# The FFN's down projection and the final norm, moved from channels on partitions to tokens on partitions

## The reference, cut to what matters

```python
h  = rmsnorm(x, norm2_g)
up = causal_dwconv(h @ ffn_w_up, conv_w, conv_b)        # 2048 -> 2 * 6144, three taps
gate, val = split(up, 2)
x  = x + (gelu(gate) * val) @ ffn_w_down                 # 6144 -> 2048
out = x * rsqrt(mean(x * x, axis=-1) + 1e-6) * final_g   # over the 2048 channels
```

## Time and profile before

| what | value |
|---|---|
| runs | 2379.47, 2385.78, 2387.15 us |
| profiled execution | 2380.07 us, span 2378.3 us |
| mean granted TensorE clock | 0.986 of full speed |
| TensorE busy | 2286.2 us (96%) |
| VectorE, ScalarE, GpSimd busy | 1311.4 us (55%), 1043.1 us (44%), 266.3 us (11%) |
| HBM read, written | 427.85 MB, 6.29 MB |

### The profile page before, as it was taken

The page is one execution under the profiler, slowest core; times in us unless marked ns, Lnnn a source line. Parts: engine busy times, 40 slices in busy tenths (PEclk is TensorE's granted clock), DMA queues, the critical chain, the costliest instruction groups (busy, mean ns, idle before and its releaser), DMA issues.

```text
span 2378.3 us, 30943 instructions
## 1 busy us (share of the span) xinstructions
PE 2286.2 (96%) x12255; PEld 1857.3 (78%) x12255; DVE 1311.4 (55%) x2114; ACT 1043.1 (44%) x1606; POOL 266.3 (11%) x333
## 2 busy tenths in 40 slices
PE   5889999999999999999999998999999999999998
PEld 2457777777777866778888886888888888888887
DVE  2443533332323264545676767667765777567764
ACT  2222333332322155445554465456544555355543
POOL 1000000000001022100010424111100110001111
PEclk9889999999999999999999999999999999999999
DMA  9764433345655465734566544555555565565552
GB/s 367 275 244 176 142 123 133 127 136 168 221 183 177 160 236 182 260 106 146 185 192 214 176 142 156 172 186 187 187 194 186 187 195 187 192 188 187 190 189 81
DMA packets 346895, 436.16 MB, mean 183 GB/s; under 512 B 13848, under 2 KB 269280, under 8 KB 345856
## 3 DMA queue, kind: packets, MB, share of 16 engines
q1 hardware_dynamic: 341376, 413.19, 52.5%
q0 software_dynamic: 3280, 15.86, 1.8%
q10 hardware_dynamic: 2096, 5.15, 0.6%
HBM read 427.85 MB, written 6.29 MB: 183 GB/s over the span
## 4 chain that ended last, share of the span: by engine, by line
PE 87%; DVE 5%; ACT 3%; DMA 3%; issue 1%; POOL 1%; SPq 0%; ACTq 0%; POOLq 0%
PE ps L1287 30%; PE ps L1288 16%; PE ps L1262 5%; PE ps L1264 5%; PE ps L1263 5%; PE ps L1282 5%; PE ps L1284 5%; PE ps L1283 5%; PE ps L1243 3%; DVE SPL L1726 2%; ACT SPL L1491 2%; DMA RAW<-in_w_in_dram 1%; PE ps L1336 1%; PE ps L1353 1%; DMA RAW<-in_ada_w_dram 1%
## 5 line engine op out<-in xcount | busy, mean ns | idle before, releaser
L1287 PE MATMUL ps<-HS,SPL 128*128 128x512 f32 x3456 | 1215.8, 396 | 14.5 <-DVE SPL L1726 9.6
L1726 DVE TENSOR_TENSOR SPL<-RAW,SPL 128x1024 fp32r<-128x1024 f32 x592 | 751.6, 1273 | 603.2 <-ACT SPL L1491 600.5
L1288 PE MATMUL ps<-HS,SPL 128*128 128x256 f32 x3456 | 968.4, 280 | 0.0
L1491 ACT ACTIVATE SPL<-RAW 128x1024 fp32r<-128x1024 f32 x592 | 621.7, 1055 | 475.1 <-PE ps L1288 281.3
L1287 PEld LDWEIGHTS ps<-HS,SPL 128*128 128x128 f32 x3456 | 649.5, 188 | 167.4 <-DVE SPL L1726 8.4
L1288 PEld LDWEIGHTS ps<-HS,SPL 128*128 128x128 f32 x3456 | 654.4, 189 | 1.9 <-issue 1.7
L1262 PE MATMUL ps<-SPL,HS 128*128 128x512 f32 x576 | 250.5, 435 | 21.1 <-ACT XT L1533 6.7
L1264 PE MATMUL ps<-SPL,HS 128*128 128x512 f32 x576 | 230.8, 401 | 0.0
L1263 PE MATMUL ps<-SPL,HS 128*128 128x512 f32 x576 | 230.8, 401 | 0.0
L1282 PE MATMUL ps<-HS,SPL 128*128 128x512 f32 x480 | 195.4, 407 | 1.2 <-DVE HS L1882 1.2
L1284 PE MATMUL ps<-HS,SPL 128*128 128x512 f32 x480 | 187.7, 391 | 0.0
(11 more groups left out here) (272 smaller groups left out, 1701.3 us busy)
## 6 DMA issues: line engine op xcount, KB each, us to landing
RAW<-in_w_in_dram SPq DMA_DIRECT2D x208, 512.0 KB, 5.8
RAW<-in_ada_w_dram SPq DMA_DIRECT2D x192, 512.0 KB, 4.9
RAW<-in_ffn_w_up_dram SPq DMA_DIRECT2D x192, 512.0 KB, 3.6
RAW<-in_w_out_dram SPq DMA_DIRECT2D x96, 512.0 KB, 4.4
RAW<-in_ffn_w_down_dram SPq DMA_DIRECT2D x96, 512.0 KB, 3.3
x_spill<-XT POOLq DMA_DIRECT2D x2, 2048.0 KB, 15.4
XT<-x_spill POOLq DMA_DIRECT2D x1, 4096.0 KB, 17.4
MM<-in_x_dram ACTq DMA_DIRECT2D x2, 1024.0 KB, 10.8
```

What stands on the lines that cost most here:

```text
L1287: mm(PS[b][:, :], wr, hh, start=k == 0, stop=False, skip_group_check=True)
L1288: m = mm(PS[b][:, 256:512], wl, hh[:, 0:256], start=False, stop=k == KT - 1, skip_group_check=True)
L1491: act(SPL[:, (n - 1) % NSPL, 0, :], raw_of(i), ACT.Copy).then_inc(s_hi, 1)
L1726: tt(w[:, 1, :], raw_of(s["i"]), w[:, 0, :].bitcast(F32), ALU.subtract).then_inc(s_lo, 1)
```

## The change: the diff

The down projection is put in tm form: four groups of 512 output channels for each round, eight chunks each, each with two banks (one for either half of the tokens). Its eviction `rows_add` adds one bank of 128 tokens by 512 channels to x. For that, x is turned at the start of the FFN: eight steps `x_turn`, put into `low`, each of four transposes into bank 7 and one copy by VectorE into `XO`, the second half of `XT`. `final_g` is no longer loaded as a row at the start; GpSimd's queue loads it at the start of the FFN, spread over all partitions (1 MB written), into `GF`, the last quarter of `MM`.

In round 2 ScalarE squares each row block of three of the four groups and sums along the row in the same instruction, and GpSimd multiplies it by the gains. The last four chunks are walked twice, first for tokens 0 to 127 and then for 128 to 255, so that the first half's norm can run beside the second half's matmuls. Of the tail there are left, for each half: the sum into x, the square, one small add, the power on GpSimd, the scaling (group 3 on VectorE with its gains, group 2 on VectorE, groups 0 and 1 on ScalarE) and four stores. The sum over partitions, the diagonal, the scaling by columns and the transposes at the end go.

```diff
-        OT = [MM[:, 2048 * t:2048 * (t + 1)] for t in range(2)]
+        XO = [XT[:, 4096 + 2048 * t:4096 + 2048 * (t + 1)].rearrange("p (g c) -> p g c", g=4) for t in range(2)]
+        GF = MM[:, 6144:8192].rearrange("p (g c) -> p g c", g=4)
...
-        c_fin2 = col(0, 80, vec(I["final_g_2"]), 16)
...
+        def x_turn(g, t):
+            def f():
+                s = put("x_turn", g=g, t=t, after=use(7), last=[y["x_done"], y["down"]], res=tick("res"))
+                bank_last[7] = [(s_res, s["res"])]
+            return f
...
+        def rows_add(r, g, banks):
+            def f():
+                ready = [rows_sum(g, t, banks[t], multiplied()) for t in range(2)]
+
+                def square(t):
+                    y["squared"] = rows_square(g, t, ready[t])
+                    put("rows_gain", g=g, t=t, last=[y["squared"]])
+                if r == 2:
+                    hi.extend([lambda: square(0), lambda: square(1)])
+            return f if (r, g) != (2, 3) else None
...
-            downs = [c for i in range(8) for c in group("fm", ("down", r), Wd, i * 256, alt(i), x_add(2 * i, alt(i), sq3 if r == 2 else None))]
+            downs = [c for i in range(4) for c in group("tm", ("down", r), Wd, i * 512, alt(i), rows_add(r, i, alt(i)), TILES[:2])]
...
+        y["x_done"] = (s_res, count["res"])
+        put("final_gain_in", last=[y["down"]])
+        low.extend([x_turn(g, t) for g in range(4) for t in range(2)])
         for r in range(3):
             need["down", r] = lambda k, r=r: [act_ready[r, k]]
-            run_chunks(marks[10 + r])
+            run_chunks(marks[10 + r] - (4 if r == 2 else 0))
             y["down"] = multiplied()
         flush(hi)
-        cnt = sq3.count(4)
-        slot, bank_last[4] = rstd_a(2, 1.0 / D, PS[4][:, 0:2], [cnt])[0], [(s_ms, count["rstd_a"])]
-        rs3 = rstd_b(2, slot, 5)
-        for k in range(KT):
-            put("final", k=k, ready=rs3, after=use(*[2 * (k // 4 % 2) + t for t in range(2)]) if k % 4 == 0 else {})
...
+        put("rows_mean", last=[y["squared"]])
+        first = at["pos"]
+        for t in range(2):
+            for kc in range(4):
+                run_ahead()
+                ks = range(2 * (4 + kc), 2 * (4 + kc) + 2)
+                put("mm", i=first + kc, c=chunks[first + kc], inputs={k: need["down", 2](k) for k in ks}, after={}, banks=[t], end=t == 1, src=None)
+                at["pos"] += t
+                at["used"] += t
+            ready = rows_sum(3, t, alt(3)[t], multiplied() if t else (s_part, tick("part")))
+            put("rows_norm", t=t, last=[rows_square(3, t, ready)], power=tick("power"), res=tick("res", 2) - 1)
...
+                elif s["kind"] == "rows_norm":
+                    t = s["t"]
+                    for sm, v, g in ((s_fine, 2 * t + 1, 0), (s_res, s["res"], 3), (s_fine, 2 * t + 2, 1), (s_res, s["res"] + 1, 2)):
+                        e.wait_ge(sm, v)
+                        e.dma_start(out[0, t * 128:(t + 1) * 128, g * 512:(g + 1) * 512], XO[t][:, g, :]).then_inc(s_out, 16)
...
+                elif kind == "x_turn":
+                    t = s["t"]
+                    for sm, v in new(*s["last"]):
+                        e.wait_ge(sm, v)
+                    for i in range(4):
+                        m = turn(PS[7][:, i * 128:(i + 1) * 128], XV[:, 0, 4 * s["g"] + i, t * 128:(t + 1) * 128], IDN[:, :])
+                    m.then_inc(s_fint, 1)
...
+                    act(T(s["slot"]), XO[t][:, g, :], ACT.Square, scale=D ** -0.5, accum_out=STAT[:, 4 * t + g:4 * t + g + 1]).then_inc(s_sqa, 1)
...
+                        act(XO[t][:, g, :], XO[t][:, g, :], ACT.Copy, scale=RSTD[:, t:t + 1]).then_inc(s_fine, 1)
...
+                    tt(o, PS[s["bank"]][:, :], o, ALU.add).then_inc(s_res, 1)
...
+                    stt(MS[:, t:t + 1], STAT[:, 4 * t + 3:4 * t + 4], EPS, STAT[:, 8 + t:9 + t], ALU.add, ALU.add).then_inc(s_ms, 1)
...
+                    stt(XO[t][:, 3, :], XO[t][:, 3, :], RSTD[:, t:t + 1], GF[:, 3, :], ALU.mult, ALU.mult).then_inc(s_res, 1)
+                    ts(XO[t][:, 2, :], XO[t][:, 2, :], RSTD[:, t:t + 1], None, ALU.mult).then_inc(s_res, 1)
...
+                    tt(RSTD[:, t:t + 1], MS[:, t:t + 1], POWS[:, 0:1], ALU.pow).then_inc(s_pow, 1)
```

More of the change, by code:

```diff
@@ L23 @@
 GATES = (8, 10, 0, 2, 4, 6, 12, 14), (8, 10, 12, 14, 0, 2, 4, 6)
-BW = [128, 120, 64, 96, 96, 96, 96]
+BW = [112, 120, 64, 96, 96, 96, 96]
 OFFS = [sum(BW[:b]) for b in range(7)]
@@ L1031, in up_out, with rows_sum, rows_square @@
             return f
+        def x_turn(g, t):
[3 more added lines that the diff above has]
+            return f
+        def rows_sum(g, t, bank, done):
+            put("rows_add", g=g, t=t, bank=bank, last=[done], res=tick("res"))
+            bank_last[bank] = [(s_res, count["res"])]
+            return bank_last[bank][0]
+        def rows_square(g, t, ready):
+            slot, last = take()
+            s = put("rows_square", g=g, t=t, slot=slot, last=[ready, *last])
+            done = (s_sqa, count["square"] + s["n"])
+            give(slot, done)
+            return done
+        def rows_add(r, g, banks):
[7 more added lines that the diff above has]
+            return f if (r, g) != (2, 3) else None
         main0, outs0, (sq0,), x0, (front0, last_out0), project0 = layer(0)
         main1, outs1, (sq1, sq1f), x1, (begin_h1, begin1), project1 = layer(1)
-        sq_gm, sq_lru, sq2, sq3 = Squares(2, 7), Squares(2, 7), Squares(2, KT - 1), Squares(2, KT - 1)
+        sq_gm, sq_lru, sq2 = Squares(2, 7), Squares(2, 7), Squares(2, KT - 1)
         left = [c for g in range(8, 12) for c in ada_group(0, g)] + [c for g in range(12) for c in ada_group(1, g)]
@@ L1259, in tensor @@
                                 else:
-                                    hr, hl = (HH[0][:, k, r, t * 128:(t + 1) * 128] for r in range(2))
+                                    half = HH[1] if stage == "down" else HH[0]
+                                    hr, hl = (half[:, k, r, t * 128:(t + 1) * 128] for r in range(2))
                                 wr, wl = (w[:, x, kk * 512:(kk + 1) * 512] for x in range(2))
@@ L1703, in scalar @@
                         act(HH[1][:, k, 0, :], GT[k % 4][:, 256:512], ACT.Copy).then_inc(s_vh, 1)
[L1705 to L1709, removed]
+                elif kind == "rows_square":
+                    t, g = s["t"], s["g"]
+                    for sm, v in new(*s["last"]):
+                        e.wait_ge(sm, v)
+                    act(T(s["slot"]), XO[t][:, g, :], ACT.Square, scale=D ** -0.5, accum_out=STAT[:, 4 * t + g:4 * t + g + 1]).then_inc(s_sqa, 1)
+                elif kind == "rows_norm":
+                    t = s["t"]
+                    e.wait_ge(s_pow, s["power"])
+                    for g in range(2):
+                        for sm, v in new((s_fin, 2 * g + t + 1)):
+                            e.wait_ge(sm, v)
+                        act(XO[t][:, g, :], XO[t][:, g, :], ACT.Copy, scale=RSTD[:, t:t + 1]).then_inc(s_fine, 1)
         def vector(e):
```

61 lines of the change are left out of this document (37 added, 24 removed).

## The result

The changed kernel takes 2367.74 us (median of 5 runs, 2366.16 to 2372.84), the kernel before on the same chip 2382.58 us (5 runs, 2376.22 to 2387.15): a ratio of 0.9942, 95% interval 0.9923 to 0.9961. That is 0.6% faster, within the range and 5.3 us under the predicted 2373. The profiled execution took 2369.71 us, 10.4 us less than that of before.

A forecast was written before the change was run, and what follows sets the result against it. TensorE was taken as the bound: matmul count times pace, plus waits, then a tail. Terms -6.9 - 2.6 + 3.5 + 5.0 - 9.2 = -10.2 us gave 2369.9 from the profile, 2375.6 from the median; forecast 2373 us, range 2363 to 2382.

The forecast's parts named there:

- The downs: Down projections: triples at 680 ns replace fm pairs, -6.9 us; the wait for VectorE's hidden layer at each start goes, -2.6.
- Turning x: Round 0's up projection: eight units of four transposes cost TensorE 0.44 us each, +3.5 us.
- The copy's wait: Round 0's up: a unit waiting for VectorE's copy of the unit before; taken as 0, at most 0.7 us a pair.
- The lock: Up projections: the pace of fm pairs is drawn anew, slow costing 3.3 us an up; +5.0 us, bounds 0 to +9.9.
- I take half: Up projections: since other entries were split about evenly, half of the +9.9 us for three slow ups, +5.0.
- The tail: After the last matmul: 16.8 us shrink to 7.6, -9.2 us; -8.4 with the slow power, -9.8 with quicker steps.
- not later than 3.4: Tail: stores starting later than 3.4 us after the last matmul would show the prediction wrong.
- I take the middle of both: Base of the sum: between 2369.9 us from the profiled execution and 2375.6 from the median, 2373 was taken.
- A: Rival: triples run at two pairs' pace (-1.6) and all three ups fall slow (+9.9); change 0.0, 2380 to 2386 us; chance 0.20.
- B: Rival: in round 0's up TensorE stalls on VectorE's copies of x, 19.6 us, about 2392 us; chance 0.06.
- C: Rival: the locks in all ups fall fast, -15.2 us, 2368 us; chance 0.07.
- stand in two pairs, 6.7 us apart: Four known executions of before, near 2380 and near 2386.5 us, read as differing by two locks of 3.3 us.

The follow-up runs named there:

- b2: The kernel before, no edit, profiled once more; that profiled execution took 2383.34 us.
- e5: The changed kernel with its fm pairs taken two by two (two matmuls of 512 columns, then two of 256): 2362.94 us, 0.992 of before.
- e6: The kernel before, without the change, with its fm pairs taken two by two: 2379.17 us, 0.9984 of before.
- b1: The kernel before, no edit, profiled once more; that profiled execution took 2381.35 us.
- e1: The kernel before plus only the eight units that turn x in round 0's up projection, their result unread: ratio 1.0017.
- a1: The changed kernel once more, no edit: 2370.91 us, ratio 0.9939 of before.

## Why the prediction was right, and where it was off

**The downs** (-6.9 and -2.6 forecast, -9.5 together): -9.43. A down is 87.07 us for 128 triples, 680 ns each, and the wait is gone. 1.5 us of it are down 2's slow pace in the profile of before, and that was its draw: b2 has this down fast (89.89 against 91.41). By the gap that the Trainium skill's page TensorE: Matmul & The Clock Gate gives (section Back-to-back issue gap) a triple would take 3 x 215.8 = 647.5 ns, an estimate, and a down 82.9 us; the trace doesn't agree, 87.07. The Trainium skill's page states that gap for a single matmul by itself; the prediction used it for a stream.

**Turning x** (+3.5 forecast): +4.1 by e5 against e6 (184.29 - 180.18), where no draw disturbs; 0.51 a unit. A unit by itself is 0.44 as forecast. The copy's wait, put at 0 to 0.7 for each pair of neighbours and taken as 0, is 0.27 at the first and near nothing at the others, of which there are three, not two; it and the 0.05 us by which the transposes last longer there make up most of the difference.

**The lock** (+5.0 forecast, half of three slow draws): +7.2 against the profiled execution: 3.40 in up 1, 3.40 in up 2, and 0.35 in up 0 (4.46 less the turns' 4.1). This step failed in its "I take half". Before ups 1 and 2 it is no draw: the hand-over from tm to fm came out slow 8 times in 8, as the only one in the trace of before had the earlier trace rows. That row was the nearest and should have carried the value; the other entries, split about evenly, were not of this kind.

**The tail** (-9.2 forecast): -9.20. That it fits to the hundredth is chance: the tail of before is 16.8 us in three profiles and 17.8 in the two where TensorE's clock fell early (b1, e1), against which it would be -10.3. The new tail has no matmul left and takes 7.55 to 7.57 us in all six profiles of its form; that the clock there no longer matters, as the prediction said, is borne out. In its parts: 2.3 us from the last matmul to the root (2.8 forecast; the power takes 0.56, less than either bound), last store issued 2.1 us later (2.1), landing after 2.0 to 2.7 us (2.2 to 2.4), 7.6 in all. The second half's first store starts 3.1 us after the last matmul, not later than 3.4.

**The sum and its base.** Own profile minus 10.2 was 2369.9, and the new profiled execution took 2369.71. That agreement is partly chance: the FFN with its tail gave -7.4, not -10.2, and the rest lies ahead of it. From the median, however, the runs moved by 14.8 us (first measurement) and 14.1 (a1). The step "I take the middle of both" is 3.1 of the 5.3 us by which 2373 came out too slow, and its reason didn't hold: the profiled execution of before had fast locks in nearly all ups, so the sum charged the change with the 353 ns pace as if before never paid for it, and then a median was used as base in which before does pay. The three profiles of before average 825.7 us for FFN and tail, 3.6 above the first, which turns -7.4 into -11.0. The 3 us left up to 14 have no place shown: executions differ by more ahead of the FFN (1548.5 to 1556.3).

**The rivals.** A: its second half came true in two ups of three, its first half not, so no zero. B: one wait of 0.2 to 0.3 us in e1 and in the changed kernel. C: its 2368 us is the time that was measured, but its mechanism fell, since no clean hand-over is fast; the agreement is chance. That executions "stand in two pairs, 6.7 us apart" as two locks was too neat: more executions fill the gap.

**What stays open.** Why a tm stream leaves the pair slow, and what in TensorE holds either pace. The runs show when, not why; the thought in e5's expectation, a weight load that comes late, is tested by no run here.

## What to carry to other kernels

Where one program's stages have a pace that is drawn anew in each execution, take two or three profiles of it before a sum is made against one, and put the sum and the median on the same draws. A hand-over that the trace shows once is better evidence for that hand-over than all other kinds of entry together. And an order of the same matmuls that showed only one pace (512, 512, 256, 256 here, three profiles) is worth trying: it took the changed kernel from 0.994 to 0.992 of before, 4.9 us of its FFN (814.7 to 809.8), for a few lines.

## What the hardware showed that was not expected

The fm pair (512 and 256 columns, each with a weight load of its own) has two paces at full granted clock, 346.7 and 353.3 ns, each held for hundreds of pairs and, where no wait and no tm stream lies between, across stages. In the fast one all pairs are alike; in the slow one three follow in turn, some 350, 360 and 350 ns (1899.79, 1900.14, 1900.50, 1900.85 and on in the kernel after). Taken two by two, pairs have one pace, 348.3 ns (178.34 us for 512), in all three profiles of that order. At the end of the kernel before, after 2.3 us without work for TensorE, eight small matmuls took 1.02 us at a granted clock of 1.00 in one execution and 1.83 at 0.50 in another. GpSimd's power of one column took 0.56 us in the tail, where the earlier trace rows has 1.46 for the same shape and the earlier trace rows 0.71 for two.
